# Gates of three blocks written by indirect transfers alone, the gate matrix zeroed earlier, and the residual loaded inside the expert stage

## The chip, the cores and the metric

The kernel runs on 1 core of one Trainium2 chip. The metric is the time on the device in microseconds (us). The kernel before took 2725.96 us, the median of 3 runs (2722.21 to 2726.33).

## The reference

Two transformer-like blocks follow one another on 512 tokens of width 1024. The first mixes tokens (gated linear attention and a state space part), then applies a product-key layer: each token picks, for each of 8 heads, 16 of 16384 single-neuron experts, so 128 slots per token. The second block mixes tokens by convolution and attention and then applies a mixture of 32 experts. The change touches the product-key layer of the first block only:

```
s = einsum('thpd,hpkd->thpk', q, sub_keys)
top_s, top_i = top_k(s, 16)                     # per head and half, of 128 keys
cand_s = top_s[:, :, 0, :, None] + top_s[:, :, 1, None, :]
best_s, best_pos = top_k(cand_s, 16)            # of 256 pairs
gate = softmax(best_s)
act = einsum('td,ted->te', x_blk, u[i_blk])
hid = gelu(act) * g_blk
out = einsum('te,ted->td', hid, v[i_blk])
h = h + out
```

## The kernel before, in words

Weights come as 1 MB chunks (128 partitions x 2048 fp32) through a ring of four buffers. ScalarE makes the bf16 high half of each chunk (`hi_in_loop`), VectorE the low half (`lo_in_loop`), three chunks ahead of TensorE, and every product is three bf16 matmuls (`mm3`: high x high, high x low, low x high). SyncE issues the chunk loads, each when VectorE has finished with the buffer.

The tokens are four blocks of 128. The product-key layer is not computed by gathering, but densely, with all 16384 experts, for blocks 1 to 3. The stage of activations (the loop over `N_U` = 64 passes, `expert_tile`) takes one chunk of `u` a pass, two tiles of 24 matmuls into PSUM banks 0 and 1, for all 512 tokens. ScalarE applies gelu to each tile (`gelu_tile`), and the result goes to `act_dram` in HBM. The stage of values (another 64 chunks) reads back the activations of blocks 1 to 3 and a matrix of gates (128 x 128 experts by tokens, mostly zero), VectorE multiplies them (`products`), ScalarE and VectorE split the product into halves, and TensorE multiplies with the chunk of `v` into banks 2 to 7, which have been loaded with the residual by six fp32 matmuls with the identity. Block 0 goes another way: GpSimd gathers its 128 activations and its 128 value rows per token by indirect transfers (`load_act`, `load_value`), and VectorE adds them up row by row (`add_row`).

The gates are found on VectorE beside the activation stage. A "unit" is one head of one block: TensorE makes its scores (`scores`, in banks 2 and 3 in turn; it waits until VectorE has read the unit before the last, `s_out`), VectorE finds the best keys (`best_keys`). Six units (`EARLY`) are made in the query projections before the stage. The units are laid into the passes by `unit_of`: eight passes with units, six without (`PERIOD` = 14). After the last unit of a block VectorE turns positions into keys (`block_slots`) and begins the softmax (`soft_start`); ScalarE makes the exponential (L1534), and VectorE ends the softmax (`soft_end`).

The gate matrix `gate_dram` is zeroed by 14 transfers on ScalarE's queue (`zero_gates`), half in the query projections and half in the first passes. The gates of blocks 1 and 2 are written into it by GpSimd, one slot of 128 tokens in one indirect transfer (`spread`, L626, 256 of them); since two slots of a token may hold the same expert, VectorE first sums equal slots (`share`, 16 slots of a head at a time, L2062) and makes the addresses (`places`), once for a block. The gates of block 3 are made otherwise: the slots are transposed (`slots`), VectorE makes one-hot matrices (`gate_one_hots`), TensorE multiplies them (`gate_tile`, 16 tiles of 8 tokens in passes 43 to 58), and ScalarE copies them out (`gates_out`); the gates of 48 tokens stay in SBUF and those of 80 go to `gate_dram` by `store_gates`, in four transfers on ScalarE's queue (L1522). GpSimd also issues the activation stores (L618), each before the spreads of its pass.

Each engine has its own list of instructions, in the order in which the code writes them, and semaphores between them; a waiting instruction holds up all that stand behind it on its engine.

Of the kernel before, what the change touches and what calls it, by code (L numbers as in the profile page):

```python
# [7 lines left out]
F32 = mybir.dt.float32  # L8
BF16 = mybir.dt.bfloat16
I32 = mybir.dt.int32  # L10
# [85 lines left out]
EARLY = 6  # L96
TD = T - P
NO_ROW = 4096
T_SPREAD = 2 * P
GT = 48  # L100
GATE_TILES = [(0, t) for t in range(0, 40, 8)] + [(1, t) for t in range(80, P, 8)] + [(0, t) for t in range(40, 80, 8)]
FIRST_TILE_AT = 43
GATE_ROW = T_SPREAD + P - GT
GATES = PK // 2 * P * 2 * GATE_ROW
ZERO_PARTS = 14
ZEROS = GATES // (P * TB * SLOTS * ZERO_PARTS)
assert GATES == ZEROS * P * TB * SLOTS * ZERO_PARTS
EARLIER = 1024.0
PERIOD = 14
SPREAD_FROM, SPREAD_PER_CHUNK = 16, 6  # L110
# [3 lines left out]
def unit_of(n):  # L114

    if n < PH - EARLY:
        return EARLY + n
    b, h = divmod(n - (PH - EARLY), PERIOD)
    return PH * (b + 1) + h if b < TB - 1 and h < PH else None


def last_unit_at(b):
    return (PH - EARLY) + PERIOD * (b - 1) + PH - 1


SOFT_AT = {last_unit_at(b) + 2: b for b in range(1, TB)}
SOFT_END_AT = {last_unit_at(b) + 3: b for b in range(1, TB)}
TURN_AT = last_unit_at(TB - 1) + 4
# [26 lines left out]
def build_program(nc, w_all, x_in, cols_in, small_in, rows_in, out):  # L155
    ctx = ExitStack()
    with ctx:  # L157
# [85 lines left out]
        g_st = view(0, 2, PK, GT)  # L243
        slot_T = view(16 * 1024, 4, P)
        o = 16 * 1024 + 4 * P
        shared = view(o, 2, SLOTS); o += 2 * SLOTS
        place = view(o, 2, SLOTS, dt=I32); o += 2 * SLOTS
# [5 lines left out]
        v_rows = [view(12 * 1024 + n * D, D) for n in range(4)] + [xn[:, n, :] for n in range(4)]  # L253
        oh_b = view(18 * 1024, 2, 8, PK, dt=BF16)
# [6 lines left out]
        oh_a = xn_flat[:, 2048:4096].bitcast(BF16).rearrange("p (r t s k) -> p r t s k", r=2, t=8, s=2)  # L261
# [6 lines left out]
        assert o <= PK * GT  # L268
# [14 lines left out]
        g_b16 = view(18 * 1024, P, dt=BF16)  # L283
# [8 lines left out]
        gate_dram = nc.dram_tensor("gate_dram", (GATES + T_SPREAD * SLOTS,), F32, kind="Internal").ap()  # L292
# [122 lines left out]
        soft_e, soft_done, slot_tp, slot_done = (sem(n) for n in ("soft_e", "soft_done", "slot_tp", "slot_done"))  # L415
        soft_shifted = lambda b: 2 * b - 1
        soft_ended = lambda b: 2 * b
        g_zero, place_done = sem("g_zero"), sem("place_done")
        oh_done, g_done, g_out = sem("oh_done"), sem("g_done"), sem("g_out")
        g_stored, g_spread = sem("g_stored"), sem("g_spread")  # L420
# [153 lines left out]
        def _(pool):  # L574
# [35 lines left out]
            for n in range(1, 4):  # L610
                load_row(n)

# [3 lines left out]
            def store_activations(n):  # L616
                pool.wait_ge(u_out, 2 * n + 4)
                pool.dma_start(act_dram[n], u_st[:, n % 2, :, :].rearrange("p j t -> p (j t)")).then_inc(u_stored[n % 2], 16)  # L618

            gate_cells = gate_dram.rearrange("(r o) -> r o", o=1)  # L620

            def spread(k):
                b, j = divmod(k, SLOTS)
                if j == 0:
                    pool.wait_ge(place_done, b + 1)
                pool.indirect_dma_start(gate_cells, bass.IndirectOffsetOnAxis(ap=place[:, b, j:j + 1], axis=0),  # L626
                                        shared[:, b, j:j + 1], None).then_inc(g_spread, 16)

            k = 0
            for n in range(N_U):  # L630
                store_activations(n)
                if n >= SPREAD_FROM:
                    for k in range(k, min(k + SPREAD_PER_CHUNK, 2 * SLOTS)):
                        spread(k)
                    k += 1
# [13 lines left out]
            for k in range(4):  # L649
                load_value(k)  # L650
# [4 lines left out]
            for k in range(4, ROWS):  # L655
                load_value(k)
# [1959 lines left out]
```

## Time and profile before

| what | value |
|---|---|
| median of 3 runs | 2725.96 us |
| profiled execution: span from the first to the last instruction | 2718.4 us |
| span, mean granted clock | 0.981 |
| TensorE busy | 2565.4 us, 94% |
| VectorE busy | 1954.2 us, 72% |
| ScalarE busy | 1228.6 us, 45% |
| GpSimd busy | 981.8 us, 36% |
| spreads (L626) | 256, 320.4 us |
| one-hots (L2121) | 256 in passes 43 to 58 |

The profile gives no time of that execution other than its span; the runs' times also hold what lies around it. A matmul's duration in the records (0.38 us) is longer than the spacing of two (0.22 us), since they are pipelined; so the spacing is what counts. Activation passes run from 350 to 1042, values from 1052 to about 1546.

### The profile page before, as it was taken

What the parts mean: (1) busy time and instruction counts of PE and PEld (TensorE: products, weight loads), DVE (VectorE), ACT (ScalarE), POOL (GpSimd) and SP (SyncE); (2) the same over time, 40 slices, a digit from 0 to 9 for tenths busy, and PEclk for the clock granted to TensorE, in tenths of its full rate; (3) what the DMA queues carried; (4) which work ended last, traced back from release to release, by engine and by line L of the source; (5) the groups of instructions that cost most, each with busy time, mean ns of one, the idle gap of its engine ahead of it and who ended that gap; (6) DMA issues with size and microseconds to landing.
All of it is one profiled execution on the core that took longest, in us unless ns stands there. A gap on an engine that the chain in (4) does not pass through costs nothing. (4 is left out here: it accounts for less than half of the span.)

```text
span 2718.4 us, 37861 instructions
## 1 busy us (share of the span) xinstructions
PE 2565.4 (94%) x13463; PEld 1277.8 (47%) x13686; DVE 1954.2 (72%) x3257; ACT 1228.6 (45%) x1284; POOL 981.8 (36%) x725
## 2 busy tenths in 40 slices
PE   7989999999999999999999899999989699999994
PEld 4465444444444444444444454455554344444441
DVE  5545888888865634888888864366544599999996
ACT  5433322323233432333333343444532488888884
POOL 0000000177777755888888400000000433334421
PEclk9989999999999999999999999999999799999997
DMA  5301774343444567999999723211214399999995
GB/s 217 109 17 55 271 273 184 146 164 140 163 155 144 161 166 281 353 364 367 364 364 364 281 109 109 93 63 65 76 63 155 129 406 394 388 404 405 406 406 211
DMA packets 175580, 610.64 MB, mean 225 GB/s; under 512 B 59360, under 2 KB 75744, under 8 KB 125792
## 3 DMA queue, kind: packets, MB, share of 16 engines
q1 hardware_dynamic: 57312, 411.62, 39.8%
q0 software_dynamic: 47712, 122.93, 12.3%
q10 hardware_dynamic: 70432, 74.46, 8.8%
q8 instruction: 76, 1.25, 0.2%
q14 instruction: 48, 0.39, 0.0%
HBM read 539.59 MB, written 73.53 MB: 226 GB/s over the span
## 5 line engine op out<-in xcount | busy, mean ns | idle before, releaser
L744 PE MATMUL ps<-a_lo,w_hi 128*128 128x512 bf16 (+2 forms) x1747 | 640.2, 369 | 3.9 <-issue 0.3
L745 PE MATMUL ps<-a_hi,w_lo 128*128 128x512 bf16 (+2 forms) x1745 | 639.4, 369 | 1.1
L743 PE MATMUL ps<-a_hi,w_hi 128*128 128x512 bf16 (+2 forms) x1698 | 621.6, 368 | 8.4 <-ACT xn L1504 2.9
L743 PE MATMUL ps<-w_hi,arena 128*128 128x512 bf16 (+1 forms) x1326 | 506.9, 382 | 31.0 <-DVE arena L2464 15.4
L745 PE MATMUL ps<-w_hi,arena 128*128 128x512 bf16 (+1 forms) x1327 | 505.1, 381 | 0.9
L744 PE MATMUL ps<-w_lo,arena 128*128 128x512 bf16 (+1 forms) x1327 | 505.1, 381 | 1.0
L2025 DVE TENSOR_TENSOR w_lo<-w_st,w_hi 128x2048 bf16<-128x2048 f32 x127 | 290.5, 2289 | 222.3 <-ACT w_hi L1498 222.3
L1498 ACT ACTIVATE w_hi<-w_st 128x2048 bf16<-128x2048 f32 x127 | 242.3, 1908 | 337.4 <-PE ps L745 317.0
L626 POOL DMA_INDIRECT gate_dram<-arena x256 | 320.4, 1252 | 85.4 <-issue 79.3
L1504 ACT ACTIVATE xn<-ps 128x512 f32<-128x512 f32 x128 | 76.1, 596 | 440.9 <-PE ps L745 440.9
L743 PEld LDWEIGHTS ps<-a_hi,w_hi 128*128 128x128 bf16 x1768 | 173.4, 98 | 193.5 <-issue 8.9
L745 PEld LDWEIGHTS ps<-a_hi,w_lo 128*128 128x128 bf16 x1768 | 173.2, 98 | 193.6
L641 POOL DMA_INDIRECT arena<-act_dram,h_idx x128 | 248.2, 1939 | 39.0 <-issue 39.0
L744 PEld LDWEIGHTS ps<-a_lo,w_hi 128*128 128x128 bf16 x1768 | 173.2, 98 | 180.9
L1773 DVE TENSOR_TENSOR w_lo<-w_st,w_hi 128x2048 bf16<-128x2048 f32 x68 | 155.0, 2287 | 121.7 <-ACT w_hi L1342 121.5
L743 PEld LDWEIGHTS ps<-w_hi,arena 128*128 128x128 bf16 (+1 forms) x1344 | 137.8, 103 | 203.5 <-DVE w_lo L2375 31.1
L745 PEld LDWEIGHTS ps<-w_hi,arena 128*128 128x128 bf16 (+1 forms) x1344 | 138.2, 103 | 154.1 <-issue 2.9
L744 PEld LDWEIGHTS ps<-w_lo,arena 128*128 128x128 bf16 (+1 forms) x1344 | 138.2, 103 | 143.1 <-issue 2.4
L669 POOL CAST arena<-xn 128x1024 bf16<-128x1024 f32 x4 | 4.1, 1036 | 544.6 <-DVE xn L1787 544.6
L1342 ACT ACTIVATE w_hi<-w_st 128x2048 bf16<-128x2048 f32 x68 | 129.0, 1904 | 97.3 <-PE ps L745 96.9
L618 POOL DMA_DIRECT2D act_dram<-xn x64 | 35.9, 560 | 337.4 <-ACT xn L1504 324.9
L2375 DVE TENSOR_TENSOR w_lo<-arena,w_hi 128x2048 bf16<-128x2048 f32 x64 | 145.9, 2280 | 13.3 <-ACT w_hi L1698 13.2
(414 smaller groups left out, 3989.7 us busy)
## 6 DMA issues: line engine op xcount, KB each, us to landing
w_st<-in_w_all SPq DMA_DIRECT2D x260, 1024.0 KB, 5.0
arena<-in_w_all SPq DMA_DIRECT2D x64, 1024.0 KB, 9.0
act_dram<-xn POOLq DMA_DIRECT2D x64, 512.0 KB, 3.1
xn<-in_w_all SPq DMA_DIRECT2D x32, 1024.0 KB, 9.0
arena<-act_dram ACTq DMA_DIRECT2D x64, 384.0 KB, 5.4
gate_dram<-xn ACTq DMA_DIRECT2D x14, 1536.0 KB, 7.9
arena<-gate_dram ACTq DMA_DIRECT2D x64, 336.0 KB, 7.4
a_hi<-in_w_all SPq DMA_DIRECT2D x16, 1024.0 KB, 8.1
```

The costliest lines, as they stand in the source:

```text
L618: pool.dma_start(act_dram[n], u_st[:, n % 2, :, :].rearrange("p j t -> p (j t)")).then_inc(u_stored[n % 2], 16)
L626: pool.indirect_dma_start(gate_cells, bass.IndirectOffsetOnAxis(ap=place[:, b, j:j + 1], axis=0), shared[:, b, j:j + 1], None).then_inc(g_ ...
L641: pool.indirect_dma_start(act_0[:, k:k + 1], None, acts, bass.IndirectOffsetOnAxis(ap=h_idx[:, k:k + 1], axis=0)).then_inc(act_ld[k // ROW ...
L743: pe.matmul(dst, l_hi, r_hi, start=start, stop=False)
L744: pe.matmul(dst, l_hi, r_lo, start=False, stop=False)
L745: return pe.matmul(dst, l_lo, r_hi, start=False, stop=stop)
L1342: act.activation(dst, w_st[:, n % RING, :], ACT.Copy).then_inc(w_hi_done, 1)
L1498: act.activation(w_hi[:, s, :], w_st[:, s, :], ACT.Copy).then_inc(w_hi_done, 1)
L1504: act.activation(u_st[:, n % 2, t, :], ps[:, t, :], ACT.Gelu).then_inc(u_out, 1)
L1773: dve.tensor_tensor(lo_n, w_st[:, n % RING, :], hi_n, ALU.subtract).then_inc(w_lo_done, 1)
L2025: dve.tensor_tensor(w_lo[:, s, :], w_st[:, s, :], w_hi[:, s, :], ALU.subtract).then_inc(w_lo_done, 1)
L2375: dve.tensor_tensor(w_lo[:, s, :], moe_st[k % MOE_RING], w_hi[:, s, :], ALU.subtract).then_inc(w_lo_done, 1)
```

## The change

All gates of blocks 1 to 3 are written by spreads (384 of them), in parts of 32 slots: the addresses of a block's slots are made after each two heads of `share`, and GpSimd starts on them. Blocks are searched in the order 1, 2, 3, 0. Seven units instead of six are made early; the last of block 1 is made in pass 0. Score units stand in passes 6 to 13, 20 to 27 and 34 to 41, shares in 1 to 4, 16 to 19 and 30 to 33. The exponential stands between the two gelus of passes 1, 15, 29 and 43. One-hots, gate tiles, the transposes of slots and the two pairs of gate stores are gone. A row of the gate matrix is 384 long instead of 336, and `products` is one instruction. The matrix is zeroed by 16 transfers that GpSimd issues in the first projections, from a zeroed part of `xn`; ScalarE waits for all of them before it writes that part (g = 2, last block). Activation stores are issued by ScalarE behind its gelus. The residual matmuls stand in passes 50 to 55, one a pass. Products and high half of the first value chunk stand ahead of the last pass's remainder and gelus. GpSimd loads eight value rows instead of four before it gathers activations.

```diff
-EARLY = 6
+EARLY = 7
+ORDER = (1, 2, 3, 0)
+BEGIN, PERIOD = 6, 14
+SOFT_AT = {last_unit_at(k) + (2 if k else 1): k for k in range(TB)}
+PARTS = 4
+RES_AT = 50
@@ gpsimd
+            pool.wait_ge(tp_done, KT)
+            pool.memset(zeros, 0.0).then_inc(const_step, 1)
+            pool.wait_ge(const_step, 4)
+            for part in range(ZERO_PARTS):
+                pool.dma_start(cells[:, part * ZEROS:(part + 1) * ZEROS, :],
+                               zeros.unsqueeze(1).to_broadcast([P, ZEROS, GATE_ROW])).then_inc(g_zero, 16)
+            load_row(3)
...
+            pool.wait_ge(g_zero, 16 * ZERO_PARTS)
+            for b in range(1, TB):
+                for j in range(SLOTS):
+                    if j % (SLOTS // PARTS) == 0:
+                        pool.wait_ge(place_done, PARTS * (b - 1) + j * PARTS // SLOTS + 1)
+                    spread(b, j)
-            pool.wait_ge(slot_done, 1)
-            for k in range(4):
+            pool.wait_ge(slots_used, 1)
+            for k in range(ROWS):
                 load_value(k)
@@ tensor
-                if 0 <= at < len(GATE_TILES):
-                    gate_tile(at)
+                if n == RES_AT:
+                    pe.wait_ge(s_out, TB * PH)
+                if RES_AT <= n < RES_AT + 6:
+                    b = n - RES_AT + 2
+                    last = pe.matmul(ps[:, b, :], ident[:, :], res[:, b // 2, (b % 2) * 512:(b % 2 + 1) * 512], start=True, stop=False)
                 expert_tile(n, 1)
-            pe.wait_ge(u_out, 2 + 2 * N_U)
-            for b in range(2, 8):
-                pe.matmul(ps[:, b, :], ident[:, :], res[:, b // 2, (b % 2) * 512:(b % 2 + 1) * 512], start=True, stop=False)
-            pe.drain().then_inc(v_done, 2)
@@ scalar
+                    if (g, tb) == (2, TB - 1):
+                        act.wait_ge(g_zero, 16 * ZERO_PARTS)
...
             for n in range(N_U):
                 hi_in_loop(n, 16 * ((C_U + n + AHEAD) // RING + 1), u_done, 2 * n + 2)
+                if n == N_U - 1:
+                    act.wait_ge(h_mul, 1)
+                    act.wait_ge(v_done, 1)
+                    products_hi(0)
                 gelu_tile(n, 0)
+                if n in SOFT_AT:
+                    k = SOFT_AT[n]
+                    gates = gate_t[:, k * SLOTS:(k + 1) * SLOTS]
+                    act.wait_ge(soft_done, soft_shifted(k))
+                    act.activation(gates, gates, ACT.Exp).then_inc(soft_e, 1)
                 gelu_tile(n, 1)
+                store_activations(n)
                 if n == N_U - 2:
+                    for b in range(TB - 1):
+                        act.wait_ge(g_spread[b], 16 * SLOTS)
                     for r in range(2):
                         load_experts(act, 0, r)
@@ vector
+            def places(b, part):
+                some = slice(part * SLOTS // PARTS, (part + 1) * SLOTS // PARTS)
+                dve.drain()
+                dve.tensor_scalar(late[:, some], shared[:, b - 1, some], EARLIER / 2, None, ALU.is_ge)
+                dve.drain()
+                dve.tensor_tensor(late[:, some], move[:, some], late[:, some], ALU.mult)
+                dve.drain()
+                dve.scalar_tensor_tensor(place[:, b - 1, some], late[:, some], float((b - 1) * P), g_at[:, some], ALU.add, ALU.add).then_inc(place_done, 1)
...
+            def products(i, c):
+                dve.wait_ge(h_ld[c % 2], 32 * (4 * i + (c // 2 + 1)))
+                dve.tensor_tensor(h_f[:, c % 2, :, :], ga_in[:, c % 2, :, :], g_in[:, c % 2, :, :], ALU.mult).then_inc(h_mul, 1)
```

## Rows read from the trace of the kernel before

**Rows 1.** Windows: busy us and instructions per engine, clock, DMA share, GB/s.
```profile
1040.00:1060.00 20.00, 15.36 (x47) 5.97 (x46) 6.70 (x9) 4.08 (x4) 11.36 (x10) 0.83 0.79 283
1200.00:1500.00 300.00, 298.47 (x1363) 135.99 (x1390) 259.05 (x244) 102.86 (x78) 252.46 (x157) 1.00 1.00 366
```

**Rows 2.** Timeline of ScalarE, gelus: start us, us, engine, line, operation [idle before].
```profile
414.46 0.60 ACT L1504 ACTIVATE xn<-ps 128x512 f32<-128x512 f32 x1 [4.52 <-PE ps L745]
...
425.15 0.60 ACT L1504 ACTIVATE xn<-ps 128x512 f32<-128x512 f32 x1 [4.52 <-PE ps L745]
...
817.10 0.60 ACT L1504 ACTIVATE xn<-ps 128x512 f32<-128x512 f32 x1 [5.84 <-PE ps L745]
...
828.36 0.60 ACT L1504 ACTIVATE xn<-ps 128x512 f32<-128x512 f32 x1 [5.42 <-PE ps L745]
...
1021.64 0.60 ACT L1504 ACTIVATE xn<-ps 128x512 f32<-128x512 f32 x1 [4.52 <-PE ps L745]
...
1032.00 0.60 ACT L1504 ACTIVATE xn<-ps 128x512 f32<-128x512 f32 x1 [4.52 <-PE ps L745]
```

**Rows 3.** Timeline of TensorE where it stood, and around the seam.
```profile
350.08 0.23 PE L743 MATMUL ps<-arena 128*128 128x128 bf16 x1 [1.57 <-DVE arena L2015]
...
1011.08 0.38 PE L743 MATMUL ps<-a_hi,w_hi 128*128 128x512 bf16 x1 [2.17 <-ACT xn L1504]
...
1043.01 5.42 PE L1057 MATMUL ps<-res,ident 128*128 128x512 f32 x12 [0.69 <-ACT xn L1504]
1052.38 0.61 PE L743 MATMUL ps<-w_hi,arena 128*128 128x512 bf16 x1 [3.95 <-DVE arena L2175]
1052.78 0.63 PE L744 MATMUL ps<-w_lo,arena 128*128 128x512 bf16 x1
...
1545.39 0.38 PE L743 MATMUL ps<-w_hi,arena 128*128 128x512 bf16 x1 [3.88 <-DVE arena L2175]
```

**Rows 4.** Timeline of VectorE: slot lists, unit, share part, block 0's rows.
```profile
371.61 0.23 DVE L1993 TENSOR_SCALAR arena<-arena 128x128 uint32<-128x128 uint32 x1
...
384.15 2.28 DVE L2025 TENSOR_TENSOR w_lo<-w_st,w_hi 128x2048 bf16<-128x2048 f32 x1
...
392.11 2.27 DVE L2025 TENSOR_TENSOR w_lo<-w_st,w_hi 128x2048 bf16<-128x2048 f32 x1
...
496.12 2.29 DVE L2025 TENSOR_TENSOR w_lo<-w_st,w_hi 128x2048 bf16<-128x2048 f32 x1
...
508.46 2.29 DVE L2025 TENSOR_TENSOR w_lo<-w_st,w_hi 128x2048 bf16<-128x2048 f32 x1
...
1069.01 0.16 DVE L2166 TENSOR_TENSOR arena<-arena,gate 128x8 f32<-128x8 f32 x1
...
1511.02 1.28 DVE L2171 SCALAR_TENSOR_TENSOR res<-arena,res 128x1024 f32<-128x1024 f32 x1 [4.04 <-DMA arena<-in_w_all,v_idx]
```

**Rows 5.** Timeline of ScalarE: last write of the projections, and an exponential's table load.
```profile
149.43 0.60 ACT L1434 ACTIVATE xn<-ps 128x512 f32<-128x512 f32 x1 [1.99 <-PE ps L745]
...
774.64 1.28 ACT L1534 ACT_TABLE_LOAD   x1
775.93 0.31 ACT L1534 ACTIVATE xn<-xn 128x128 f32<-128x128 f32 x1
```

**Rows 6.** Timeline of GpSimd: a spread beside VectorE's remainder; gathers of activations.
```profile
992.54 2.94 POOL L626 DMA_INDIRECT gate_dram<-arena  x1 [0.30 <-issue]
...
1051.80 1.35 POOL L641 DMA_INDIRECT arena<-act_dram,h_idx  x1 [0.30 <-issue]
...
1062.83 0.95 POOL L641 DMA_INDIRECT arena<-act_dram,h_idx  x1 [0.30 <-issue]
```

**Rows 7.** Windows: a stretch with weight loads alone, and one with zeroing.
```profile
60.00:70.00 10.00, 9.95 (x50) 4.97 (x50) 9.11 (x10) 3.11 (x4) 0.00 (x0) 1.00 0.30 107
...
300.00:320.00 20.00, 19.89 (x101) 9.44 (x102) 16.16 (x51) 5.99 (x6) 0.00 (x0) 1.00 0.70 250
```

**Rows 8.** Groups of instructions: the spreads, busy us, mean ns, idle before.
```profile
L626 POOL DMA_INDIRECT gate_dram<-arena x256 | 320.4, 1252 | 85.4 <-issue 79.3 <-DVE arena L2089 6.1
```

More of the change, by code:

```diff
@@ L117, in unit_of, with last_unit_at @@
         return EARLY + n
[L118 to L128, printed above, removed]
+    k, h = divmod(n - BEGIN, PERIOD)
+    return PH * (k + 1) + h if 0 <= k < TB - 1 and h < PH else None
+def last_unit_at(k):
+    return BEGIN + PERIOD * (k - 1) + PH - 1 if k else PH - EARLY - 1
+SOFT_AT = {last_unit_at(k) + (2 if k else 1): k for k in range(TB)}
+SOFT_END_AT = {last_unit_at(k) + (3 if k else 1): k for k in range(TB)}
+SHARE_AT = {ORDER[k]: n for n, k in SOFT_END_AT.items()}
+PARTS = 4
+RES_AT = 50
 ROWS = 8
@@ L1022, in expert_tile @@
                 last.then_inc(u_done, 1)
-            def gate_tile(at):
-                pe.wait_ge(oh_done, at + 1)
-                pe.wait_ge(g_out, 2 * at + 2)
-                for r in range(8):
-                    dst = ps[:, 2 + 2 * (at % 2) + r // 4, (r % 4) * PK:(r % 4 + 1) * PK]
-                    pe.matmul(dst, oh_b[:, at % 2, r, :], oh_a[:, at % 2, r, 0, :], start=True, stop=False)
-                    last = pe.matmul(dst, oh_b[:, at % 2, r, :], oh_a[:, at % 2, r, 1, :], start=False, stop=True)
-                    if r % 4 == 3:
-                        last.then_inc(g_done, 1)
             pe.wait_ge(ft_out, F_QUERY + 2 * N_QUERY)
@@ L1504, in gelu_tile @@
                 act.activation(u_st[:, n % 2, t, :], ps[:, t, :], ACT.Gelu).then_inc(u_out, 1)
-            def gates_out(at):
-                b, first = GATE_TILES[at]
-                first -= 80 if b else first // 40 * 40
-                if at == 11:
-                    act.wait_ge(g_stored, 32)
-                for bank in range(2):
-                    act.wait_ge(g_done, 2 * at + bank + 5)
-                    tok = slice(first + bank * 4, first + bank * 4 + 4)
-                    act.activation(g_st[:, b, :, tok].rearrange("p k t -> p t k"),
-                                   ps[:, 2 + 2 * (at % 2) + bank, :].rearrange("p (t k) -> p t k", t=4), ACT.Copy).then_inc(g_out, 1)
@@ L1517, in store_gates, with store_activations @@
-            def store_gates(tiles, first):
-                act.wait_ge(g_out, 4 + 2 * tiles)
-                by_pair = g_st[:, 0, :, 0:40].rearrange("p (n j) t -> p j n t", j=2)
-                for j in range(2):
-                    at = j * GATE_ROW + T_SPREAD + first
-                    act.dma_start(gate_rows[:, :, at:at + 40].rearrange("n p t -> p n t"), by_pair[:, j, :, :]).then_inc(g_stored, 16)
+            def store_activations(n):
+                act.wait_ge(u_out, 2 * n + 4)
+                act.dma_start(act_dram[n], u_st[:, n % 2, :, :].rearrange("p j t -> p (j t)")).then_inc(u_stored[n % 2], 16)
@@ L1557, in expert_values @@
-                if not isinstance(i, int) or c < 7:
-                    hi_in_loop(c, 16 * (C_V // RING + 2 * i + ((c + AHEAD) // RING + 1)), v_done, 8 * i + (c + 2))
-            with act.Fori(0, N_V // 8 - 1) as i:
+                products_hi(c)
+                next_weights(i, c)
+            next_experts(0, 0)
+            next_weights(0, 0)
+            for c in range(1, 8):
+                expert_values(0, c)
+            with act.Fori(1, N_V // 8 - 1) as i:
                 for c in range(8):
```

231 lines of the change are left out of this document (73 added, 158 removed).

## The prediction

> **What bounds the kernel now.** I read the windows first, then each engine's timeline at the seams, then the DMA rows. In the stage of expert values TensorE is busy for 298.47 of 300 us, with VectorE at 259 and DMA at share 1.00; the seam between the expert stages, 1040 to 1060, is the weak place: 15.36 of 20 us busy, at a mean clock of 0.83 [rows 1]. So nearly all of the stretch that the change touches is set by TensorE, and time can come only from matmuls taken away, from TensorE's own waits, and from the clock. The busy engines beside it (VectorE, GpSimd) cost only where they become late.
>
> One pass of the activation stage, from one gelu to the same gelu of the next pass, is 10.36 us without anything added (1021.64 to 1032.00), 10.69 with a score unit (414.46 to 425.15) and 11.26 with a gate tile (817.10 to 828.36) [rows 2]. The stage runs from 350.08 to the 1042.2 at which the last tile ends, then come 0.7 us of idle, 5.42 us of fp32 residual matmuls, and 3.95 us of idle until 1052.38. The first matmuls there start 0.40 to 0.43 us apart, where 0.22 is full speed: half the 2.4 GHz clock, for about 12 matmuls, 2.5 us [rows 3].
>
> **The sum, part by part** (TensorE's time, from 350 to the stage behind the values):
>
> 1. Gate tiles, 16 of them, go: 16 x (11.26 - 10.36) = -14.4. With them go the three transposes and the wait for the first tile, about -0.7 (estimate from the same gelu spacing).
> 2. The two stores of gates on ScalarE's queue go. Behind one of them TensorE stood 2.17 us waiting for a gelu [rows 3]; the two are alike: -4.3.
> 3. The six residual matmuls move into passes 50 to 55. They cost the same 5.42 us there: +5.4 here, and they leave the seam (below). Their banks 2 to 7 are free once the scores are read.
> 4. One score unit moves from pass 0 to the last query part: -0.3, since TensorE idles 1.57 us at 350.08 anyway, waiting for the low half of a query [rows 3].
> 5. But that unit puts 5.7 us of VectorE work in front of pass 0 (a unit with its weight remainder is 384.15 to 392.11, 7.96, less 2.2 for the remainder [rows 4]). VectorE was to start pass 0 at 352; now it does so at 355.6, runs unit 7 until 363.5, then the block's slot lists, 371.61 to 384.15 = 12.5 us [rows 4], and offers the shifted scores at 376.4. New is that ScalarE waits for them in pass 1 between its two gelus, with a table load of 1.28 us on each side of the exponential [rows 5]: the second gelu ends at 376.4 + 1.28 + 0.31 + 1.28 + 0.6 = 379.9, and TensorE wants that bank at 376.3. Queued behind the waiting exponential are this gelu, the activation store and the next weight conversion. Stall: +3.6 (bounds 0, if the lists were ready 4 us earlier, and 5).
> 6. VectorE's backlog. A share part with its remainder is 496.12 to 508.46 = 12.34 us [rows 4]; with the new small operations on 32 columns (three, with drains, an estimate of 0.8 from such short gaps as lie between the rows) 13.1, against 10.36 of TensorE. From 376.4: pass 1 costs 17.4 (softmax end, start of share, cells, first part), passes 2 to 4 13.2 each, pass 5 2.2: VectorE starts unit 8 at 435.6. TensorE is at pass 8 at 437.7, and its scores there need the banks that unit 8 has read at 439.7: +2.0 (bounds 0 and 5). The weight remainder of pass 8 is ready at 435.6, just in time. In blocks 2 and 3 the share begins level with TensorE, and the same sum gives about +0.4 each. This replaces a stall of 0.6 of the same kind in the present kernel.
>    Third share: VectorE loses the one-hots of 16 tiles and gains 128 share slots; both lie beside matmuls.
> 7. Chance of half clock after the gap of 3.6: a gap of 3.88 us (1545.39) was followed by it, one of 2.17 was not [rows 3]. Half of about 1.7: +0.9.
>
> Items 1 to 7: -14.4 - 0.7 - 4.3 + 5.4 - 0.3 + 3.6 + 2.8 - 0.6 + 0.9 = -7.6.
>
> 8. The seam. Now 0.7 + 5.42 + 3.95 + 2.5 = 12.7 us between the last activation tile and full speed (about; 10.2 to the first value matmul). After the change products and high half of chunk 0 are made before the last pass's gelus, so the value matmuls can follow at once: 0.3, and 0.5 for the chance that its loads land late. What is late next is block 0: GpSimd may gather activations only once the last ones are stored, some 4 us behind the last tile; eight gathers took 1051.80 to 1062.83 [rows 6], the last of them had landed at most 6.2 later, when VectorE used it at 1069.01 [rows 4]. That is 21 us after the last tile; VectorE is ready for them at 15, and its queue holds two rows, a remainder and then the low half of chunk 3, which TensorE wants at 23.8. With 5 us of landing I get +2.5 (bounds 0.5 and 5) and +0.9 for the clock. 12.7 - 4.2: -8.5.
> 9. End of the values: GpSimd has the first eight value rows early, so it is 8 us further ahead of VectorE than now. At 1511.02 VectorE waited 4.04 us for a row [rows 4], and TensorE stood 1.8 and 3.88 us behind it. I take -2.0 (bounds 0 and -4).
>
> **Costed at nothing, and by what cover.** Zeroing: 16 transfers of the same 1.57 MB as the present 14 (only 1536-byte instead of 2048-byte runs), issued by GpSimd from about 19.5; ScalarE must have them by its write at 149.43 [rows 5]. Beside one weight chunk per pass the DMA share is 0.30; with one zero transfer added it is 0.70 [rows 7], so a transfer takes 0.40 x 10.36 = 4.1 us of all engines, 66 in all, 87 if it goes by the run. With 0.7 left over that ends between 114 and 144. Spreads: 384 at (320.4 + 79.3) / 256 = 1.56 us [rows 8] from 394 (first addresses, by item 6) end at 993; the loads of pass 62, some 10 us before the last tile's end at 1042.2 - 7.6, need them at about 1025. The issue of activation stores by ScalarE: beside matmuls, ScalarE being idle for over half of a pass. Gate rows of 384 instead of 336: 48 KB more per chunk beside 2.8 MB; TensorE sets the pace there. The products as one instruction spare VectorE some 0.1 us a chunk.
>
> Sum: -7.6 - 8.5 - 2.0 = -18.1. The profiled execution has a span of 2718.4, and the median of the runs lies 7.6 above it; I leave that difference as it is: 2725.96 - 18.1 = 2707.9, say 2708. With the bounds of items 5, 6, 8 and 9 (about +5.5 and -9) its own range is 2699 to 2715.
>
> **Rivals.**
>
> A. The zeroing is late (slower than before). The transfers go through GpSimd, and there is no row of a direct GpSimd transfer with 1024 runs; the gathers and spreads with 128 took 0.95 to 2.94 us of issue. At 7.6 us of issue each (eight times 0.95) the last lands near 150 and nothing is lost; from 9.2 us each the end at 168 eats the whole gain; at 9.9 it is 178, TensorE stands 28 us, and the time is 2708 + 28 = 2736. For it: GpSimd instructions are stretched whenever VectorE's remainder runs (the spread at 992.54 took 2.94) [rows 6]. Against: a run costs far less in a direct transfer than in an indirect one if the issue is one description. 8 in 100.
>    By the Trainium skill (SBUF — State Buffer, Who interferes with whom) the descriptors of a GpSimd transfer are written by GpSimd itself and starve while VectorE holds their common port, which a transfer from ScalarE's queue does not; that speaks against moving the zeroing, and the trace's stretched spread agrees. By it this rival would have more weight, since VectorE is half busy in that stretch.
>
> B. The spreads end late (slower). From 1.65 us each instead of 1.56 (they now also meet the shares of three blocks) the loads of pass 62 wait; at 1.75 they end at 1066 and cost 41 - 10 (the slack in pass 63): 2739. For it: 1.56 is a mean over a stretch with much VectorE work. Against: the present kernel also spends issue time on 64 stores. 4 in 100.
>
> C. The value stage is set by DMA. 2816 instead of 2768 KB a chunk at share 1.00: 1.7% of 490 us, +8.5: 2716. For it: the share [rows 1]. Against: TensorE's 298.47 of 300, so the share holds slack. 10 in 100.
>
> D. The stalls of items 5, 6 and 8 don't arise: 2708 less the 9 of those lower bounds and the 2 of the clock = 2697. 12 in 100.
>
> E. The backlogs are worse than reckoned: VectorE's lag at pass 8 is also a late weight remainder, and each such stall brings half clock: +12, 2720. 8 in 100.
>
> My forecast has 58 in 100. Less than 0.2% (5.5 us) can't be told from no change here. Faster: forecast, C and D wholly, most of E: 0.82. Same: part of E, early cases of A and B: 0.07. Slower: A, B: 0.11. For 8 in 10 the range takes in D and C and part of E: 2696 to 2722.
>
> **What would show it.** The first value matmul within 1 us of the last activation tile, and the half clock at the seam gone or moved to chunk 3 with a VectorE wait for gathered activations before it (item 8). A TensorE wait of some 3.6 us on a gelu in pass 1, one of 2 us on VectorE's key search in pass 8 (items 5, 6). Passes 43 to 58 at 10.36. The last zero landing before 150, with no ScalarE wait there; the last spread near 993. I am wrong if TensorE stands at 150 or at pass 62, if the spacing of the value matmuls grows, or if the stalls in passes 1 to 8 sum to over 10 us.

## The result, and the profile after

| | time, us (median, lowest to highest) | against the kernel before, same chip |
|---|---|---|
| before | 2724.35 (2722.21 to 2726.33) | |
| changed | 3031.81 (2994.13 to 3067.2) | 1.1085 [1.1046, 1.1123] |

The forecast was 2708, range 2696 to 2722, so the change misses it by over 320 us, on the other side of the time before. Medians are of all runs, while the ratio, here and in all tables below, is of fast runs alone, which leaves out runs of over 1.5% above the fastest of the same kernel (here the one of 3067.2). The profiled execution took 3030.71 us, with a span of 3029.1.

Windows of the changed kernel show where the time went. The columns are: stretch, its length, then busy us (and count) of PE, PEld, DVE, ACT and POOL, then TensorE's clock, DMA share and GB/s.

```profile
360.00:400.00 40.00, 37.02 (x171) 16.64 (x172) 36.86 (x138) 14.51 (x14) 6.13 (x5) 1.00 0.30 106
400.00:440.00 40.00, 17.59 (x64) 6.07 (x64) 12.80 (x74) 2.51 (x2) 30.80 (x31) 0.76 0.14 40
440.00:480.00 40.00, 6.34 (x13) 1.39 (x14) 4.58 (x26) 0.60 (x1) 27.57 (x29) 0.50 0.02 1
...
520.00:560.00 40.00, 33.66 (x151) 14.77 (x154) 30.88 (x111) 9.32 (x9) 25.00 (x20) 0.83 0.42 145
560.00:600.00 40.00, 39.79 (x201) 18.88 (x204) 28.72 (x104) 11.14 (x12) 19.11 (x16) 1.00 0.42 148
...
960.00:1000.00 40.00, 8.85 (x16) 1.67 (x16) 8.29 (x38) 0.00 (x0) 26.93 (x27) 0.50 0.02 2
```

Three stretches, about 405 to 528, 660 to 790 and 920 to 1040, have TensorE at 6 to 9 of 40 us busy, VectorE and ScalarE idle too, almost nothing on the DMA engines, and the clock at 0.50, the 1.2 GHz level, after TensorE had fallen idle. Only GpSimd is busy: about 30 instructions in 40 us, the indirect spreads of one block. Outside the three stretches the stage runs as planned (560 to 600). The last activation store is issued at 1356.0, where the kernel before has its last at 1045.9; that is the whole loss (the span is 310.7 us longer).

The waits of 405 to 520 (engine and line, what it waited for: us, times, longest) say what kind of stop it is. "issue" is a wait that no semaphore in the profile ends.

```profile
ACT xn L1470 <- remote: 104.1, 3, 52.7
DVE arena L2022 <- issue: 59.0, 24, 11.2
PEld ps L734 <- issue: 39.7, 16, 6.3
PEld ps L736 <- issue: 33.2, 15, 3.4
...
POOL gate_dram L620 <- issue: 25.6, 84, 0.3
```

The timeline inside the stop (start, us, engine, line, operation, idle before):

```profile
423.49 0.59 PE L735 MATMUL ps<-a_lo,w_hi 128*128 128x512 bf16 x1 [0.83 <-issue]
424.23 0.96 POOL L620 DMA_INDIRECT gate_dram<-arena  x1 [0.30 <-issue]
...
425.50 0.96 POOL L620 DMA_INDIRECT gate_dram<-arena  x1 [0.31 <-issue]
425.58 0.58 PE L736 MATMUL ps<-a_hi,w_lo 128*128 128x512 bf16 x1 [1.49 <-issue]
...
427.02 0.35 DVE L2022 SCALAR_TENSOR_TENSOR arena<-arena 128x128 f32<-128x128 f32 x1 [6.74 <-issue]
...
427.68 0.59 PE L734 MATMUL ps<-a_hi,w_hi 128*128 128x512 bf16 x1 [1.52 <-issue]
...
459.96 0.35 DVE L2022 SCALAR_TENSOR_TENSOR arena<-arena 128x128 f32<-128x128 f32 x1 [11.18 <-issue]
...
476.75 0.18 DVE L2048 TENSOR_SCALAR arena<-arena 128x32 f32<-128x32 f32 x1 [11.17 <-issue]
```

Matmuls of one tile, whose operands all lie ready, start 2.1 us apart (423.49, 425.58, 427.68), where [rows 3] have 0.40 at the same clock. Nearly all their distances in the stop are multiples of 0.70 (1.40, 2.10, 2.80, 3.50). VectorE gets its instructions in bursts with up to 11.2 us between. GpSimd goes on, a spread every 1.27 us. ScalarE only follows: its row "remote" is the gelu waiting for TensorE's tile, and the trace's semaphore events have each gelu of this stop start within 0.1 us of the end of its tile. So TensorE and VectorE don't wait for data or for each other, but for their next instruction. I call such a stretch a stop.

How a stop ends says what holds it up. GpSimd runs out of addresses at 522.8, and TensorE is back at an even spacing from 528.7, at the full clock from 533.3:

```profile
521.81 0.96 POOL L620 DMA_INDIRECT gate_dram<-arena  x1 [0.30 <-issue]
532.29 2.76 POOL L620 DMA_INDIRECT gate_dram<-arena  x1 [9.52 <-DVE arena L2052]
```
```profile
526.61 0.59 PE L736 MATMUL ps<-a_hi,w_lo 128*128 128x512 bf16 x1 [1.52 <-issue]
...
528.70 0.58 PE L735 MATMUL ps<-a_lo,w_hi 128*128 128x512 bf16 x1
529.08 0.63 PE L736 MATMUL ps<-a_hi,w_lo 128*128 128x512 bf16 x1
...
533.28 0.38 PE L734 MATMUL ps<-a_hi,w_hi 128*128 128x512 bf16 x1
```

In this profile and in that of the unaltered kernel on chip E (below) all six stops end 3 to 9 us after GpSimd has fallen silent, in pauses of 7.1 us or more. Four pauses of 3.9 to 5.5 us inside the stops ended none.

A version with a wait for a pass ahead of every seventh spread (below, "seven per pass", 2704.93 us on its chip) has no stop and shows what the rest of the change does. Its windows, its waits of TensorE from 345 to 1120, and its seam:

```profile
400.00:540.00 140.00, 136.38 (x652) 63.48 (x664) 119.52 (x450) 43.08 (x42) 106.65 (x86) 0.99 0.44 155
...
1060.00:1080.00 20.00, 16.89 (x65) 7.15 (x67) 17.10 (x14) 3.64 (x4) 16.34 (x13) 0.83 0.78 265
1200.00:1500.00 300.00, 298.47 (x1362) 135.99 (x1390) 258.16 (x206) 101.44 (x78) 252.56 (x156) 1.00 1.00 371
```
```profile
PE ps L737 <- DVE arena L2112: 5.2, 2, 4.9
PE ps L737 <- DVE arena L1932: 5.0, 3, 2.8
PE ps L737 <- ACT xn L1473: 2.8, 1, 2.8
```
```profile
1033.95 0.38 PE L739 MATMUL ps<-a_hi,w_lo 128*128 128x512 bf16 x1
1034.67 0.39 PE L737 MATMUL ps<-w_hi,arena 128*128 128x512 bf16 x1 [0.33 <-DVE arena L2112]
...
1056.95 0.17 DVE L2103 TENSOR_TENSOR arena<-arena,gate 128x8 f32<-128x8 f32 x1 [8.27 <-DMA arena<-act_dram,h_idx]
```

The first value matmul starts 0.72 us after the last activation matmul, where [rows 3] have 10 us with the residual matmuls in it; the value stage is as full as in [rows 1].

### The profile page after: what moved, and what is told of

Read it like the earlier page. It is cut to its first block and busy times, and to the rows that moved or that the text cites. A ratio compares the mean times of both kernels' runs of the same rounds, so it can differ in the third digit from the quotient of the medians.

```text
span 3029.1 us, 37379 instructions
## 1 busy us (share of the span) xinstructions
PE 2614.3 (86%) x13205; PEld 1268.0 (42%) x13427; DVE 1922.7 (63%) x3222; ACT 1210.9 (40%) x1255; POOL 1052.7 (35%) x806
## 3 DMA queue, kind: packets, MB, share of 16 engines
q8 instruction: 74, 1.21, 0.2%
## 5 line engine op out<-in xcount | busy, mean ns | idle before, releaser
L734 PE MATMUL ps<-a_hi,w_hi 128*128 128x512 bf16 (+3 forms) x1705 | 636.5, 376 | 99.0 <-issue 81.1
L736 PE MATMUL ps<-a_hi,w_lo 128*128 128x512 bf16 (+3 forms) x1741 | 650.1, 376 | 73.0 <-issue 71.2
L735 PE MATMUL ps<-a_lo,w_hi 128*128 128x512 bf16 (+2 forms) x1745 | 651.6, 376 | 71.0 <-issue 66.8
L620 POOL DMA_INDIRECT gate_dram<-arena x384 | 414.1, 1078 | 419.5 <-DVE arena L2052 290.4
L1464 ACT ACTIVATE w_hi<-w_st 128x2048 bf16<-128x2048 f32 x127 | 242.8, 1911 | 352.6 <-PE ps L736 305.3
L634 POOL DMA_INDIRECT arena<-act_dram,h_idx x128 | 240.2, 1877 | 238.7 <-issue 238.7
L2022 DVE SCALAR_TENSOR_TENSOR arena<-arena 128x128 f32<-128x128 f32 x384 | 113.9, 349 | 198.7 <-issue 195.3
L638 POOL DMA_INDIRECT arena<-in_w_all,v_idx x128 | 161.8, 1264 | 91.7 <-DVEq L2065 53.0
L2105 DVE SCALAR_TENSOR_TENSOR res<-arena,res 128x1024 f32<-128x1024 f32 x128 | 164.4, 1284 | 13.1 <-issue 3.0
```

What stands on the lines that cost most here:

```text
L634: pool.indirect_dma_start(act_0[:, k:k + 1], None, acts, bass.IndirectOffsetOnAxis(ap=h_idx[:, k:k + 1], axis=0)).then_inc(act_ld[k // ROW ...
L638: pool.indirect_dma_start(v_rows[k % ROWS], None, values_in, bass.IndirectOffsetOnAxis(ap=v_idx[:, k:k + 1], axis=0)).then_inc(row_in[k % ...
L734: pe.matmul(dst, l_hi, r_hi, start=start, stop=False)
L735: pe.matmul(dst, l_hi, r_lo, start=False, stop=False)
L736: return pe.matmul(dst, l_lo, r_hi, start=False, stop=stop)
L1464: act.activation(w_hi[:, s, :], w_st[:, s, :], ACT.Copy).then_inc(w_hi_done, 1)
```

## Experiments

Each group below ran on one chip, and each group on another; the kernel before took 2721.3, 2722.7, 2723.0, 2725.4 and 2722.5 us in them (medians). I call the chips A to E. Which of them, if any, was the first comparison's isn't known. All kernels are built from the changed one; the code shown is cut to the lines that differ.

### Chip A: the spreads taken away, tied to passes, bounded, moved

**No spreads.** `spread(b, j)` is not called.

> Leaves out the 384 spreads (the gate matrix of blocks 1 to 3 stays zero); everything else of the changed kernel is kept. In the changed kernel TensorE nearly stops three times, from about 412 to 528, 673 to 790 and 929 to 1040 us, always while GpSimd issues spreads 1.27 us apart. Theory A (the spreads' issue itself starves the other engines) and every rival that blames the spreads: the stops are gone, 2700 to 2715 us. If the loss has another cause (gelus waiting for the stores that ScalarE now issues, VectorE's shares), it stays near 3030.

Measured 2704.02 us, 0.9930 [0.9912, 0.9949].

**Seven per pass.**
```diff
+                    k = (b - 1) * SLOTS + j
+                    if k % 7 == 0:
+                        pool.wait_ge(u_out, 2 * (4 + k // 7) + 4)
                     spread(b, j)
```


> The changed kernel, but each group of 7 spreads waits for the gelu of a pass (pass 4 on), as the kernel before did with 6; stores stay on ScalarE. Theory A (an unbroken row of spreads is what starves the others, a pause of 1 to 2 us per pass ends it): 2705 to 2725. Rival B (it is the activation stores on ScalarE's queue that come late): near 3030, as nothing of that is changed. Rival C (it is spreads beside VectorE's share instructions, which now overlap): still slow in the passes with shares, 2 to 4 passes per block, 2750 to 2900.

Measured 2704.93 us, 0.9929 [0.9911, 0.9948], no stop. But the wait hardly paced the spreads. Behind the long wait for the first addresses it held GpSimd six times, for 5.0 us in all, and GpSimd made rows of 85, 128 and 128 spreads with 0.30 us between the end of one and the start of the next. The wait of GpSimd for a gelu, 380 to 1060 us:

```profile
POOL gate_dram L620 <- ACT xn L1473: 144.4, 7, 139.4
```

**Four in flight.** Four semaphores in turn for the landings, and a spread waits for the fourth before it.

> The changed kernel, but a spread waits until the fourth one before it has landed, so that at most 4 are in flight; no other pacing. Theory A: never a backlog, so no stop, 2705 to 2725 with the spreads further apart than 1.27 us. If it is the number of spreads per time and not the backlog, the stops stay in part. Rival B: near 3030. Rival C: slow in the passes with shares.

Measured 2706.41 us, 0.9934 [0.9918, 0.9951], no stop.

**After the shares.**
```diff
-                    if j % (SLOTS // PARTS) == 0:
-                        pool.wait_ge(place_done, PARTS * (b - 1) + j * PARTS // SLOTS + 1)
+                    if j == 0:
+                        pool.wait_ge(place_done, PARTS * b)
```


> The changed kernel, but the spreads of a block start only when all four parts of its places are there, so that no spread runs beside a share instruction; 128 then follow each other with no wait. Theory A: 128 in a row are 163 us, so the stops come after the shares instead and last as long or longer, 3000 us or more. Rival C (the overlap with the shares): no stop, 2705 to 2730.

Measured 2712.88 us, 0.9970 [0.9958, 0.9981], no stop, though 384 spreads run unpaced from 433 to 1022, also beside the shares of blocks 2 and 3. On this chip, then, no unpaced row stops the others; since the unaltered kernel wasn't run on it, that says nothing yet of what makes a stop on another.

### Chip B: shorter rows, no stores, plain transfers

**Rows of eight, rows of sixteen.** `if k and k % 8 == 0: pool.wait_ge(g_spread[0], 16 * k)` ahead of the spread, one semaphore for all; 16 in the second.

> The changed kernel, but after every 8 spreads GpSimd waits until all of them have landed; no other pacing, so the spreads still run beside the shares. In the runs so far no unbroken row of spreads (starts 1.27 us apart) was longer than 10 where TensorE kept its pace, and every stop of the changed kernel lies in rows of 13 to 49. Theory A2 (an unbroken row of more than about 10 is what stops the others): no stop, 2700 to 2712. Rival C (spreads beside shares, however they are spaced) has lost with the kernels of 7 per pass and of 4 in flight; if it is the mean rate that counts (8 in about 12.3 us here against 7 in 10.4), part of the stops stays, above 2750.

> The same with a wait after every 16 spreads. Theory A2: a stop begins in each row but ends with it, since the wait for the landing gives the others a pause; the changed kernel needed no more than the pause of about 10 us at 522 to recover. 2740 to 2950. If rows of 16 do no harm, 2700 to 2712, and what counts is something that takes longer to build up than 20 us.

Measured 2783.56 us, 1.0231 [1.0203, 1.0258], and 2734.18 us, 1.0040 [1.0028, 1.0052]. Neither has a stop up to 1020. Both lose at the seam: the last spread starts at 1094.3 and at 1051.9, the first loads of the values wait for it, and TensorE stands. That is rival B of the prediction:

```profile
1108.04 0.61 PE L737 MATMUL ps<-w_hi,arena 128*128 128x512 bf16 x1 [72.04 <-DVE arena L2111]
```
```profile
1065.72 0.61 PE L737 MATMUL ps<-w_hi,arena 128*128 128x512 bf16 x1 [28.47 <-DVE arena L2111]
```
(TensorE's timeline at the seam, rows of 8 and rows of 16.)

The row lengths in the expectation (10, and 13 to 49) count spreads whose starts are 1.27 us apart, so a spread stretched beside VectorE's weight remainder ends a row. In a stop VectorE makes few remainders, and by this count rows grow long because of the stop. Counted by GpSimd's pauses, the changed kernel has rows of up to 64, and kernels without a stop have them of up to 128 (chips A, B and D). Below, a row is counted by the pauses.

**No stores.** ScalarE's activation stores of passes 4 to 63 go.

> The changed kernel without the activation stores of passes 4 to 63 (in their place eight GpSimd transfers fill that part of the activations with ones during the first projections, after the zeroing, so the values are wrong); spreads unpaced. Theory A2: the stops stay, 2980 to 3060, because the spreads do it alone and the gelus' waits for stores are only a consequence. Rival B (ScalarE's stores coming 11 to 14 us late hold the gelus, TensorE behind them): the stops are gone or much smaller, under 2800.

Measured 2708.91 us, 0.9948 [0.9931, 0.9964], no stop. A poor experiment: GpSimd's fill held its queue, so that only 4 spreads ran before 437, past the first block's shares. It was done again below.

**Plain transfers.** `pool.dma_start` of the same column to neighbouring cells in place of the indirect form.

> The changed kernel with each indirect spread replaced by a plain GpSimd transfer of the same column (128 elements of 4 bytes, to 128 neighbouring spare cells; the gate matrix stays zero), as unpaced as before. If the stops come from any unbroken row of GpSimd transfers of 4-byte elements: they stay, or are worse as a plain transfer is issued faster (0.57 us for a store), about 3000. If they belong to the indirect form (addresses worked out by GpSimd): 2700 to 2715.

Measured 2737.11 us, 1.0044 [1.0020, 1.0068]: neither of the two. TensorE is only 2.74 us busy from 460 to 480, and a gelu waited up to 24.2 us for an activation store. That is not a stop as above: the DMA share is 0.99 in that stretch, where it was 0.02 in 440 to 480 of the changed kernel, and the wait is for a transfer. So this edit put another limit in place of the one that it was to test.

### Chip C: what in GpSimd's stream matters

By now kernels with a wait far behind had shown no stop although their first 13 spreads ran just as those of the changed kernel. So I looked for the cause in the stream itself.

**One semaphore.** `then_inc(g_spread[0], 16)` for all.

> The changed kernel with one semaphore for the landings of all 384 spreads in place of one for each block; no wait is added. The kernel with a wait after every 16 spreads ran its first 13 spreads at the very times of the changed kernel (first spread + 2.5, 3.8, 5.1 us and so on) and beside the same share instructions, yet VectorE did not stall 10 us after the first spread as it does in the changed kernel. It differed up to there only in the semaphore and in the instructions that follow in GpSimd's stream. Theory D (what GpSimd's stream holds behind the running spreads counts, its waits): with the semaphore alone changed the stops stay, 2980 to 3060. Theory E (the semaphores' use counts): no stops, 2700 to 2715.

**Met waits.** `if j % 16 == 0: pool.wait_ge(g_zero, 16 * ZERO_PARTS)` ahead of the spread, but for the very first.

> The changed kernel with 23 more waits in GpSimd's stream, one before every 16th spread, on a semaphore that has its value long before: they never hold GpSimd, they only stand in its stream. Theory D1 (a real pause every 16 spreads is needed): stops stay, 2980 to 3060. Theory D2 (when GpSimd fetches its next instructions, which any added instruction moves, against VectorE's fetch): the stops go in some or all blocks, 2700 to 2900. Theory E: stay.

**Drains before.** `for _ in range(40): pool.drain()` ahead of the first spread.

> The changed kernel with 40 drain instructions on GpSimd ahead of the first spread, in the 127 us in which it waits for the first places anyway. Nothing within the rows of spreads is changed but where in them GpSimd's instruction fetches fall. Theory D2: the stops change their place or go, 2700 to 2950. Theory D1 and E: as the changed kernel, 2980 to 3060.

**Two parts first.** The wait is for `min(j * PARTS // SLOTS + 2, PARTS)` parts.

> The changed kernel, but a quarter of a block's spreads starts when also the next quarter of the places is there, so that GpSimd begins a row some 13 us later against VectorE's shares and seldom stands at a wait for places within a row. Theory F (the stop needs GpSimd at an unmet wait for VectorE's places while spreads are under way): fewer or no stops, 2700 to 2850. Theory D2: may go or stay. If neither waits nor position count, 2980 or more.

| | us | against before |
|---|---|---|
| one semaphore | 3049.8 (2962.1 to 3113.1) | not given: its runs scatter by 150 us |
| met waits | 3080.72 | 1.1308 [1.1244, 1.1371] |
| drains before | 3068.33 | 1.1204 [1.1120, 1.1287] |
| two parts first | 3109.18 | 1.1441 [1.1416, 1.1467] |

All four stop in each of the three blocks. VectorE's first late instructions come 11 to 14 us after the first spread. Separate semaphores, 23 waits that don't hold, 40 drains ahead of the row and another starting point beside the shares don't prevent the stops. This pointed to a real pause (D1), though "after the shares" on chip A had run without one.

The last of the four also shows that no share has to run beside the spreads. Its last share of the second block is over at 732.7 us, TensorE is 37.85 of 40 us busy from 740 to 780, and then comes a stop, 788 to 888:

```profile
800.00:840.00 40.00, 10.24 (x18) 1.80 (x18) 0.00 (x0) 0.60 (x1) 30.42 (x32) 0.50 0.02 0
```

The one kernel of 32 between waits, next, can't be told from "one semaphore" up to its 33rd spread.

### Chip D: how long a row, which start, which neighbours

**Rows of 32**, as rows of 8 above; **first two gated**: `if j in (8, 16): pool.wait_ge(g_spread[0], 16 * ((b - 1) * SLOTS + j))`.

> The changed kernel with a wait for the landings after every 32 spreads (so at each quarter of a block's places). Rows of 16 showed no stop, unpaced rows did, from the ninth spread on. If what counts is how many spreads GpSimd still has ahead of it when it runs unpaced, and 32 is enough: stops again, 2850 to 3080. If it takes more than 32 in a row: 2700 to 2735.

> The changed kernel with a wait for the landings only after the 8th and the 16th spread of each block; the other 112 of a block are unpaced. If a stop can start only with the first spreads after GpSimd has stood idle: no stop, 2700 to 2715, and two waits a block would be all the repair that it needs. If it can start in any unpaced row beside the shares: stops begin after the 16th spread, some 20 us later than in the changed kernel, 2950 to 3060.

Measured 2710.89 us, 0.9947 [0.9929, 0.9966], and 2709.18 us, 0.9947 [0.9928, 0.9965]; no stop in either, though the second has rows of 97 and 82 spreads. In the first there is none even in the 20 us in which "one semaphore" on chip C had already fallen into its own.

**No shares.** The loop of share instructions becomes one `memset` of `shared` to EARLIER.

> The changed kernel without VectorE's 384 share instructions (each gate is marked as already dealt with, so every spread goes to spare cells); spreads unpaced, each block's with a fresh start. If VectorE's shares beside the row are needed for a stop: no stop, 2690 to 2710 (less VectorE work than in any other). If the unpaced row does it alone: three stops, 2950 to 3060.

**No stores, again**, with the fill behind the last spread.

> The changed kernel without the activation stores of passes 4 to 63; eight GpSimd transfers behind the last spread fill that part of the activations with ones, which ends the first stage some 30 to 60 us late, so only the stretch up to about 1040 us counts. If ScalarE's stores are needed for a stop: none, a time of 2730 to 2770 by the fill. If not: three stops as in the changed kernel, above 3000.

Measured 2718.70 us, 0.9984 [0.9970, 0.9997], and 2812.56 us, 1.0330 [1.0310, 1.0350]. Neither stops; the second loses 107.38 us at the seam by its fill. All four kernels of this chip run without a stop, and all four of chip C with three. That made the chip itself the suspect, and these two experiments worthless for what they were to show: nothing says that this chip would have stopped the unaltered kernel. Without shares, ScalarE spent 13.0 us and TensorE's weight loads 20.0 us in "issue" waits between 380 and 1020, but the DMA share is 0.94 there (0.42 in rows of 32), and ScalarE's gelus waited 151.9 us for activation stores. So that kernel, too, has another limit in it.

### Chip E: the unaltered change and seven per pass, side by side

> The changed kernel, not altered. If the stops belong to the kernel wherever it runs (pacing is the cause): 2990 to 3070 again. If they belong to some chips only: on a chip without them 2700 to 2716, the kernel's own time without stops as the kernels with waits far apart show it (2709, 2711).

> The kernel of 7 spreads per pass once more, beside the unaltered changed kernel on the same chip. Pacing is the cause: 2700 to 2710 here while the other stops. The chip is the cause: both near 2705, or both above 2950.

| | us | against before |
|---|---|---|
| changed kernel, unaltered | 3047.68 (3014.05 to 3102.63) | 1.1148 [1.1096, 1.1199] |
| seven per pass | 2746.30 (2743.79 to 2748.34) | 1.0080 [1.0067, 1.0093] |

Windows of the two, the unaltered one first:

```profile
400.00:540.00 140.00, 50.96 (x157) 16.17 (x158) 40.03 (x205) 9.31 (x9) 99.47 (x97) 0.60 0.13 40
660.00:800.00 140.00, 55.20 (x151) 15.91 (x153) 39.75 (x205) 9.17 (x9) 98.55 (x98) 0.56 0.11 34
920.00:1060.00 140.00, 52.94 (x160) 16.15 (x162) 40.14 (x199) 9.20 (x9) 99.55 (x97) 0.60 0.11 36
```
```profile
400.00:540.00 140.00, 135.04 (x642) 62.29 (x653) 116.03 (x425) 40.68 (x41) 97.60 (x80) 0.98 0.45 157
540.00:560.00 20.00, 13.40 (x59) 5.79 (x58) 9.67 (x66) 4.56 (x5) 12.47 (x13) 0.92 0.14 50
700.00:780.00 80.00, 66.96 (x300) 30.06 (x305) 61.05 (x327) 18.41 (x18) 52.80 (x48) 0.91 0.32 108
```

On one chip, with nothing else changed, the wait for the pass takes 3047.68 - 2746.30 = 301 us away (291 by the ratios). Both halves of the suspicion are true: how the spreads are let go is a cause, and the chip matters as well, since the same kernel of seven per pass is 41 us slower here than on chip A (2704.93) while the kernel before differs by 1. What is left here is the same thing in small. Waits of seven per pass, 380 to 1060, on chip E:

```profile
POOL gate_dram L620 <- ACT xn L1473: 186.7, 17, 140.8
...
DVE w_lo L1989 <- issue: 27.8, 5, 8.3
PEld ps L737 <- issue: 26.4, 34, 7.0
DVE arena L2025 <- issue: 19.5, 13, 5.6
```

On this chip the wait does hold GpSimd: 16 times after the first, 45.9 us in all, against 6 times and 5.0 us on chip A. It does so when TensorE is late, since it waits for the gelu of a pass. At 537 to 555 GpSimd makes 14 spreads 1.27 us apart, while TensorE drops to 13.40 of 20 us; then the pass is missing, GpSimd pauses 4.0 us, and TensorE's tile is done 2.5 us into that pause. So the wait works as a brake that a stop pulls on itself, and not as an even pace.

The length of a row by itself isn't what counts here either. On this chip, rows of 63 spreads (from 620.4) and of 95 (from 818.3), with 0.30 us between them, leave TensorE at 79.63 of 80 and at 139.65 of 142 us:

```profile
620.00:700.00 80.00, 79.63 (x383) 37.01 (x389) 64.07 (x175) 27.22 (x27) 64.48 (x50) 1.00 0.46 159
818.00:960.00 142.00, 139.65 (x634) 63.15 (x643) 55.65 (x87) 42.13 (x41) 113.05 (x95) 1.00 0.41 145
```

The two dips lie where the shares of a block run (540 to 602 and 703 to 767). Chip C has stops without shares, so a share isn't needed; that shares help a stop to begin isn't shown.

**What is shown and what is open.** Shown: the loss lies in the stops, in each of the three blocks; in them TensorE and VectorE lack instructions while GpSimd goes on; they end when GpSimd's spreads pause for 7 us or more; on a chip that has them, a wait that holds the spreads to the passes removes all but 24 us of the 325 by which the unaltered kernel is above the time before; separate semaphores, waits that don't hold and the starting point don't prevent them, and no share has to run beside the spreads for one to begin or to last. Open: what the spreads take from the others (no row names it, and the DMA engines are nearly idle); what starts a stop, as rows of 63 and 95 did no harm on chip E; why chips differ; whether chips A, B and D would stop the unaltered kernel, which wasn't run there; and so also whether ScalarE's stores or the indirect form are needed, and whether any edit tried on A, B or D cures anything. Every kernel that stopped ran on C or E or in the first comparison.

## Why the prediction was wrong

**The step that failed** is the one sentence on spreads under "Costed at nothing". It priced them by GpSimd's time alone, 384 x 1.56 us from 394 to 993, and took the work beside it as cover. They were issued from 392.41 on, as reckoned, and in the stops 1.27 us apart, faster than reckoned. What they cost was the other engines' time: 3031.81 less the 2705 to 2711 us of versions without stops on other chips, 321 to 327 us, and 301 us on the one chip where both were run. The sum had no term for one engine's issue slowing another's, and no rival had one. In the kernel before, the 256 spreads of [rows 8] stand in 44 rows of at most 6, each followed by a pause of 0.9 to 4.5 us that has the pass's activation store in it; the change takes those stores and pauses away and makes rows of up to 64. I read the mean (1.56 us) and not how the spreads stood in the passes. That this is the difference that matters is supported by chip E alone.

The rest, from seven per pass on chip A (span 2702.5, profile of before 2718.4):

- **Items 1, 2: right.** Passes without unit or residual matmul are 10.36 throughout, and the gate tiles' and stores' stalls are gone.
- **Item 3: right.** Passes 50 to 55 take 11.22, so 6 x 0.86 = 5.2 against 5.4.
- **Item 5: right in place,** 2.8 us of waiting for the gelu of pass 1 against 3.6.
- **Item 6: right in place, too small.** VectorE's key search held TensorE three times, 5.0 us against 2.8, the longest 2.8 in pass 8.
- **Item 7: half clock came once, but elsewhere.** The clock stayed at 1.00 after the 2.8 us in pass 1, for which it was charged, and fell after the 2.8 us in pass 8 (0.91 in 430 to 450).
- **Items 1 to 7 together:** from TensorE's wait at the start to the last activation tile 347.49 to 1034.3 = 686.8 us, before 350.08 to 1042.2 = 692.1: -5.3 against -7.6.
- **Item 8: the seam closed** as said (0.72 us), and block 0 became late next as said; but TensorE stood 4.9 us, not 2.5. GpSimd's first gather started at 1041.8, 7.5 us behind the last tile and not 4, and VectorE got the activations at 1056.95, 22.6 us behind it against 21 reckoned. The half clock followed (0.83 in 1060 to 1080).
- **Item 9:** a wait of 4.3 us stays near the end (1531.26), of 5.7 before: -1.4 against -2.0. Items 8 and 9 together, from the last tile to the second group of transposes behind the values (1544.45, before 1557.83): 510.2 against 515.6, -5.5 against -10.5.
- **Sum:** -10.8 of the predicted -18.1 in that stretch. The stage also starts 2.6 us earlier in this profile than in that of before, which in the profile of the kernel without spreads it does not, so that part is spread between executions. In medians on chip A the gain is 16.3 us, 2704.93 against 2721.28. That is near the forecast of 18 in part by luck, since items 1 to 9 gave only 10.8 of it.
- **Rival A (zeroing late): false.** In the changed kernel itself the 16 transfers were issued in some 0.9 us each, the last at 114.0 us after a wait of 82.1 of GpSimd, and TensorE was at 79.42 of 80 us from 20 to 100:

```profile
20.00:100.00 80.00, 79.42 (x389) 38.45 (x395) 52.25 (x58) 37.05 (x44) 11.87 (x14) 1.00 1.02 398
100.00:120.00 20.00, 19.79 (x151) 10.47 (x151) 6.09 (x5) 10.99 (x14) 0.90 (x1) 1.00 0.83 317
```

- **Rival B (spreads late)** arose only where I slowed them (rows of 8 and 16): waits of 72 and 28 us at the seam. For spreads that end at 1095 and 1053 its sum (the end less 1025, less 10) gives 60 and 18, so it had the mechanism right and the size some 10 us too small.
- **Rival C (values set by DMA): false,** 298.47 of 300 us as before.

## What to carry to other kernels

Where many small GpSimd transfers are merged into one stream, look at what broke that stream up in the kernel that works, and keep something of it: a wait for the pass costs next to nothing while TensorE is on time (chip A: 2704.93 us, against 2704.02 without any spreads) and holds GpSimd back when TensorE is late. On the chip that had stops it gave back 301 us. A safe number of transfers in a row isn't shown: 95 did no harm on the chip where the unaltered kernel stopped. "Issue" waits on several engines at once beside idle DMA engines mean that instructions come late; no chain of semaphores shows the culprit, but what each stop's end follows does. And put the unaltered kernel on the chip of its variants, and ask of each variant whether its edit took hold: here the overlap, the stores and the start of a row each looked needed only because the chips differed, and the "pace" of chip A was hardly one.

## What the runs showed of the hardware, unexpected

- Instructions of TensorE and VectorE can come late for over 100 us while the DMA engines are at share 0.02: matmul starts at multiples of 0.70 us, bursts of VectorE instructions up to 11.2 us apart. By the Trainium skill (Runtime: NRT & Kernel Launch, Instruction fetch mechanics) each engine streams its instructions by a DMA queue of its own, in blocks of 16 KiB, and that is mostly hidden. The page of the changed kernel has two such queues (74 packets, 1.21 MB, and 50 packets, 0.41 MB, so 16 and 8 KB a packet). But the stops are not a wait for these packets as far as they are recorded. The 16 KB queue has one packet for about 120 matmuls and as many weight loads of TensorE, across the first stop (415.07 to 543.38) as before it (383.20 to 415.07). From 450 to 525 us neither queue has a packet, and yet TensorE makes 31 matmuls and VectorE 63 instructions, late; and TensorE is back at full speed before the packet of 543.38. What delays the instructions stays open. The two queues in 400 to 540 us, in the changed kernel and then in seven per pass on chip A:

```profile
q8 instruction: 1, 0.02, 0.0%
q14 instruction: 2, 0.02, 0.0%
```
```profile
q8 instruction: 6, 0.10, 0.3%
q14 instruction: 6, 0.05, 0.1%
```
- The same skill (SBUF — State Buffer, Who interferes with whom) knows one conflict, VectorE's and GpSimd's common port, and leaves TensorE out. The trace has that conflict (the spread at 410.21 took 2.29 us beside the remainder at 409.39, 0.96 otherwise); the stops are another, as TensorE is in them.
- Chips differ in it by 41 us for one kernel (2704.93 and 2746.30) while they agree within 4.1 us on the kernel before.
